# First gate-up of a two-block layer: raw tokens with shift columns for three passes, full modulated tokens after

## What is computed

```python
def modulate(h, shift, scale):
    return h * (1.0 + scale) + shift

def swiglu(h, w_in, w_out):
    gate, up = jnp.split(h @ w_in, 2, axis=-1)
    return (jax.nn.silu(gate) * up) @ w_out

# in the block, with sh_f, sc_f from silu(c) @ w_ada + b_ada:
h = modulate(rms_norm(x, g_pre_ffn), sh_f, sc_f)
x = x + gt_f * rms_norm(swiglu(h, w_ffn_in, w_ffn_out), g_post_ffn)
```

## Time and profile before

| | us |
|---|---|
| median of 3 runs | 965.96 |
| lowest and highest run | 964.58, 970.26 |
| the profiled execution's own time | 967.7 |
| its span in the profile | 965.9 |

### The profile page before, as it was taken

One profiled execution on the slowest core, in us unless ns is written; L12 is line 12 of the kernel. 1 busy time (PEld: TensorE's weight loads), 2 busy tenths in 40 slices (PEclk: granted clock), 3 DMA queues, 4 the chain that ended last, 5 costly groups with the idle time before them and its releaser, 6 DMA issues.

```text
span 965.9 us, 19407 instructions
## 1 busy us (share of the span) xinstructions
PE 951.5 (99%) x7543; PEld 883.8 (92%) x7543; DVE 639.9 (66%) x995; ACT 494.6 (51%) x762; POOL 68.7 (7%) x100
## 2 busy tenths in 40 slices
PE   8999999999999999999999999999999999999997
PEld 3776778899999999899999999999999999999997
DVE  4788886687666765765555546665778766666554
ACT  4765647664454543554444434645665554444531
POOL 0012002200000021000000000200210100000000
PEclk9999999999999999999999999999999999999999
DMA  9972447546666795266666744663445557667741
GB/s 359 400 259 89 131 133 241 185 162 198 183 187 182 207 303 152 67 196 176 179 181 178 224 119 125 214 187 109 129 135 168 160 177 215 188 181 208 220 137 43
DMA packets 189183, 176.06 MB, mean 182 GB/s; under 512 B 7312, under 2 KB 177824, under 8 KB 188752
## 3 DMA queue, kind: packets, MB, share of 16 engines
q1 hardware_dynamic: 183456, 154.29, 52.8%
q0 software_dynamic: 4960, 17.64, 5.2%
q10 hardware_dynamic: 720, 3.49, 0.9%
HBM read 174.32 MB, written 1.05 MB: 182 GB/s over the span
## 4 chain that ended last, share of the span: by engine, by line
PE 85%; DVE 9%; ACT 3%; issue 1%; DMA 1%; SPq 1%; DVEq 0%; ACTq 0%
PE acc L2007 24%; PE acc L2009 23%; PE acc L2008 23%; DVE lo L1143 2%; PE acc L2400 1%; DMA slab_hi<-in_w_ada 1%; PE acc L2205 1%; ACT hi L621 1%; PE acc L2207 1%; PE acc L2206 1%; PE wk L2007 1%; PE acc L2136 1%; PE wk L2009 1%; PE wk L2008 1%; PE wk L2136 1%
## 5 line engine op out<-in xcount | busy, mean ns | idle before, releaser
L1143 DVE TENSOR_TENSOR lo<-raw,hi 128x1024 fp32r<-128x1024 f32 (+1 forms) x259 | 331.0, 1288 | 209.4 <-ACT hi L621 209.1
L621 ACT ACTIVATE hi<-raw 128x1024 fp32r<-128x1024 f32 (+1 forms) x260 | 283.2, 1098 | 130.2 <-PE acc L2009 125.3
L2007 PE MATMUL acc<-n_high,hi 128*128 128x272 f32 (+3 forms) x1016 | 291.2, 287 | 0.5 <-DVE n_low L1958 0.3
L2008 PE MATMUL acc<-n_low,hi 128*128 128x272 f32 (+3 forms) x1016 | 288.1, 284 | 0.0
L2009 PE MATMUL acc<-n_high,lo 128*128 128x272 f32 (+3 forms) x1016 | 288.0, 283 | 0.0
L2007 PEld LDWEIGHTS acc<-n_high,hi 128*128 128x128 f32 (+1 forms) x1016 | 191.7, 189 | 3.0 <-issue 1.4
L2008 PEld LDWEIGHTS acc<-n_low,hi 128*128 128x128 f32 (+1 forms) x1016 | 191.3, 188 | 0.5
L2009 PEld LDWEIGHTS acc<-n_high,lo 128*128 128x128 f32 (+1 forms) x1016 | 191.3, 188 | 0.2
L2007 PE MATMUL acc<-g_high,hi 128*128 128x256 f32 (+1 forms) x528 | 149.2, 283 | 0.0
L2009 PE MATMUL acc<-g_high,lo 128*128 128x256 f32 (+1 forms) x528 | 148.9, 282 | 0.0
L2008 PE MATMUL acc<-g_low,hi 128*128 128x256 f32 (+1 forms) x528 | 148.7, 282 | 0.0
(11 more groups left out here) (428 smaller groups left out, 1246.1 us busy)
## 6 DMA issues: line engine op xcount, KB each, us to landing
raw<-in_w_in SPq DMA_DIRECT2D x52, 512.0 KB, 4.1
raw<-in_w_ffn_in SPq DMA_DIRECT2D x44, 512.0 KB, 3.7
raw<-in_ffn_w_gate SPq DMA_DIRECT2D x44, 512.0 KB, 3.8
raw<-in_ffn_w_up SPq DMA_DIRECT2D x44, 512.0 KB, 3.8
raw<-in_ffn_w_down SPq DMA_DIRECT2D x32, 704.0 KB, 4.5
stage<-in_w_late POOLq DMA_DIRECT2D x24, 512.0 KB, 4.8
raw<-in_w_ffn_out SPq DMA_DIRECT2D x16, 704.0 KB, 5.9
raw<-in_w_out SPq DMA_DIRECT2D x16, 512.0 KB, 4.2
```

Source lines behind the costliest of these rows:

```text
L621: act.activation(hi[:, j, 0:width], raw[:, j, 0:width], ACT.Copy).then_inc(hi_ready, 1)
L1143: dve.tensor_tensor(lo[:, j, 0:width], raw[:, j, 0:width], hi[:, j, 0:width].bitcast(F32), ALU.subtract).then_inc(lo_ready, 1)
L2007: pe.matmul(out_, wH, xH, start=start, stop=False)
L2008: pe.matmul(out_, wH, xL, start=False, stop=False)
```

## The change

In `gu0`, passes 0 to 2 (`RAW_ITS = 3`) stay as they are. From pass 3 on the tokens that are streamed are the full modulated ones, `R * gmod * inv + shift`, 256 columns wide, from `mixH` and `mixL`. They are made in passes 1 and 2: for each of the eight 128-row tiles VectorE makes `R * gmod * inv` in `xg` (`token`), ScalarE adds the shift and rounds (`token_upper`, an Identity with a bias), VectorE makes the lower half (`token_lower`). Passes 3 to 10 then need no column copy, no inverse norm and no bias: ScalarE takes the Silu straight from the accumulator (`gate`), VectorE multiplies (`product`). The engines' orders are written out anew. Since `mixH` and `mixL` are now in use, GpSimd's pieces go to `stage2`, in the memory of the raw tokens, and their first loads wait until pass 2 is done. Counts of `nl_ready`, `sg_ready` and others further on are shifted by constants.

The core of the diff, cut:

```diff
+RAW_ITS = 3
...
-            pool.wait_ge(mm_done, 4 * BASE["gu0"])
+            pool.wait_ge(mm_done, 4 * BASE["gu0"] + 12)
             stage_half(12)
             stage_half(13)
...
+            def token_upper(k):
+                act.wait_ge(xn_ready, KD + k + 1)
+                act.activation(mixH[:, k, :], xg[:, k, 0:T], ACT.Identity, bias=mods[:, 24 + k, 0:1]).then_inc(nh_ready, 1)
...
             def gate_up_shifted(name, ahead):        # ScalarE
...
+                def gate(i):
+                    multiplied(name, i, 1)
+                    act.activation(sg[:, :, 0:T], acc[:, 0:2, 0:T], ACT.Silu).then_inc(acc_free[0], 1)
+
+                def inner_upper(i):
+                    act.wait_ge(acc_free[1], USE[name] + i + 1)
+                    act.activation(inner(g_high, T)[:, ds(2 * i, 2), :], hbuf[:, :, 0:T], ACT.Copy).then_inc(gh_ready, 1)
+
+                for j in (1, 2, 3):
+                    split(first + 1, j, 1024)
+                raw_gate(0)
+                raw_inner(0)
+                for i in (1, 2):
+                    split(first + i + 1, 0, 1024)
+                    token_upper(4 * i - 4)
+                    token_upper(4 * i - 3)
+                    split(first + i + 1, 1, 1024)
+                    raw_gate(i)
+                    split(first + i + 1, 2, 1024)
+                    token_upper(4 * i - 2)
+                    token_upper(4 * i - 1)
+                    split(first + i + 1, 3, 1024)
+                    raw_inner(i)
+                with act.Fori(RAW_ITS + 1, n) as i:
+                    act.activation(warm[:, 7:8], ident[0:1, 0:1], ACT.Silu)
+                    split(first + i, 0, 1024)
+                    split(first + i, 1, 1024)
+                    gate(i - 1)
+                    split(first + i, 2, 1024)
+                    split(first + i, 3, 1024)
+                    inner_upper(i - 1)
...
+            def token(k):
+                dve.scalar_tensor_tensor(out=xg[:, k, 0:T], in0=R[:, k, FRAMES], scalar=gmod[:, k, 2:3], in1=inv[:, 0:T],
+                                         op0=ALU.mult, op1=ALU.mult).then_inc(xn_ready, 1)
+
+            def token_lower(k):
+                dve.wait_ge(nh_ready, 25 + k + 1)
+                dve.scalar_tensor_tensor(out=mixL[:, k, :], in0=xg[:, k, 0:T], scalar=mods[:, 24 + k, 0:1],
+                                         in1=mixH[:, k, :].bitcast(F32), op0=ALU.add, op1=ALU.subtract).then_inc(nl_ready, 1)
+
             def gate_up_shifted(name, ahead):        # VectorE
...
+                def product(i):
+                    multiplied(name, i, 3)
+                    dve.wait_ge(acc_free[0], USE[name] + i + 1)
+                    dve.wait_ge(lo_ready, 4 * (BASE[name] + i) + 5)
+                    dve.tensor_tensor(hbuf[:, :, 0:T], acc[:, 2:4, 0:T], sg[:, :, 0:T], ALU.mult).then_inc(acc_free[1], 1)
+                    inner_lower(i)
+
+                split(first + 1, 1, 1024)
+                raw_gate(0)
+                split(first + 1, 2, 1024)
+                raw_inner(0, lambda: split(first + 1, 3, 1024))
+                for i in (1, 2):
+                    split(first + i + 1, 0, 1024)
+                    token(4 * i - 4)
+                    token(4 * i - 3)
+                    split(first + i + 1, 1, 1024)
+                    token_lower(4 * i - 4)
+                    token_lower(4 * i - 3)
+                    raw_gate(i)
+                    split(first + i + 1, 2, 1024)
+                    token(4 * i - 2)
+                    token(4 * i - 1)
+                    split(first + i + 1, 3, 1024)
+                    token_lower(4 * i - 2)
+                    token_lower(4 * i - 1)
+                    raw_inner(i)
+                with dve.Fori(RAW_ITS + 1, n) as i:
+                    for j in range(4):
+                        split(first + i, j, 1024)
+                    product(i - 1)
...
             def gate_up(name, t0, width, behind, first, steps, operands=(mH, mL), later=None):     # TensorE
...
+                if later:
+                    for s in range(2):
+                        pair(g + 2, USE[name] + 2, s, *xs, width)
+                    xs, width = later, T
+                    pair(g + RAW_ITS, USE[name] + RAW_ITS, 0, *xs, width, (nl_ready, 25, 1))
+                    pair(g + RAW_ITS, USE[name] + RAW_ITS, 1, *xs, width)
+                with pe.Fori(RAW_ITS + 1 if later else 2, COUNT[name]) as i:
```

More of the change, by code:

```diff
@@ L360, in program, with stage_tile @@
         LINEAR_AT = {1: 0, 3: 1}
+        def stage_tile(n, b):
+            side = SLAB_AT[n][0]
+            return stage2[:, 2 * side + b, 0:1024] if n >= 12 else stage[:, 2 * b + 1 - side, :]
         def head_bank(n):
@@ L937, in gate_up_shifted, with raw_gate, raw_inner @@
-                pipeline(name, 1024, evac, ahead, silu=True, behind=((0,), (1,), (), (2, 3)), shifted=True)
+                first, n = BASE[name], COUNT[name]
+                def raw_gate(i):
+                    act.wait_ge(acc_free[0], USE[name] + i + 1)
+                    for m in range(2):
+                        ins = act.activation(sg[:, m, 0:T], sg[:, m, 0:T], ACT.Silu, bias=bcol[:, m, :])
+                    ins.then_inc(sg_ready, 1)
+                def raw_inner(i):
+                    act.wait_ge(hb_ready, i + 1)
+                    act.activation(inner(g_high, T)[:, 2 * i:2 * i + 2, :], hbuf[:, :, 0:T], ACT.Copy).then_inc(gh_ready, 1)
@@ new lines, in gate_up_shifted @@
+                with act.Fori(RAW_ITS + 1, n) as i:
[6 more added lines that the diff above has]
+                    inner_upper(i - 1)
+                split(first + n, 0, ahead[0])
+                gate(n - 1)
+                split(first + n, 1, ahead[1])
@@ L939, in gate_up_scaled @@
+                inner_upper(n - 1)
+                split(first + n, 2, ahead[2])
+                split(first + n, 3, ahead[3])
             def gate_up_scaled(name, f, width, ahead):
@@ L1677, in gate_up_scaled @@
                 pipeline(name, 1024, evac, ahead, peel=True, behind=((0,), (), (), (1, 2, 3)))
-            def gate_up_shifted(name, ahead):
[L1680 to L1703, removed]
@@ L1749, in next_tokens @@
             def next_tokens(k):
-                scaled_lower(25, k, TM, 0, gain(N_F1, k))
+                scaled_lower(33, k, TM, 0, gain(N_F1, k))
             post_norm(3, 4, next_tokens, TM)
@@ L2450, in _, with gate_up @@
             HALVES = [(4 * q + kk, s) for q in range(2) for s in range(2) for kk in range(4)]
-            def gate_up(name, t0, width, behind, first, steps, operands=(mH, mL)):
+            def gate_up(name, t0, width, behind, first, steps, operands=(mH, mL), later=None):
                 xs = (lambda k: operands[0][:, k, t0:t0 + width], lambda k: operands[1][:, k, t0:t0 + width])
@@ L2506, in _ @@
             pe.wait_ge(ada_used, 1)
-            gate_up("gu0", 0, T + 2, lambda: sum_squares(2, T), 17, PACED)
+            gate_up("gu0", 0, T + 2, lambda: sum_squares(2, T), 17, PACED,
+                    later=(lambda k: mixH[:, k, :], lambda k: mixL[:, k, :]))
             down("dn0", 0, T)
```

65 lines of the change are left out of this document (44 added, 21 removed).

## The result

| us | before | after |
|---|---|---|
| median (21 runs each) | 966.17 | 970.04 |
| lowest and highest | 961.71, 970.26 | 966.79, 976.21 |
| the profiled execution's own time | 967.7 | 969.3 |
| its span | 965.9 | 967.4 |

After over before is 1.005 (95% interval 1.0038 to 1.0062), a loss of 3.7 to 6.0 us. The forecast was +7.6: the direction was right, the size too large.

The account below looks back on a forecast made before the run. TensorE, busy 951.5 of 965.9 us, was taken to bound the kernel. Waits 10.1, less 2.3 for width and 0.2 at the down projection, gave +7.6 us: 973.6 on the median, range 966.5 to 979.5.

Parts of the forecast that it names:

- The waits: TensorE idles four times in passes 2 and 3 of the first gate-up, for accumulators and the seventh token: 10.1 us together.
- The chain: VectorE and ScalarE handing to and fro in passes 1 and 2: 16.9 us a pass, against 11.6 for TensorE.
- Work alone fills VectorE: In passes 1 and 2, token instructions add 3.2 to 3.8 us a pass to VectorE's 7.90 busy of 11.60.
- The rival without waits: Engines take ready instructions ahead of blocked ones in the first gate-up, so only the saving is left: 963.5 us; chance 0.07.
- The saving by width: From pass 3 on, 256 columns instead of 258: eight passes of 96 matmuls at 3.0 ns less, 2.3 us.
- The faster-spacing rival: A pause may leave 113.1 ns spacing in passes 4 to 10 and the down projection, gaining 3.2 and 2.5 us: 967.9; chance 0.16.
- The lower clock: Rival: TensorE's clock falls after the two longest waits, 5.8 us for one, 11.6 for both: 979.4 to 985.2; chance 0.12.
- is dense again at once: Argument against the lower-clock rival: the TensorE cover that hides the passes resumes densely right after a wait; no size given.
- The signs named in advance: Right: four idles of 2 to 3 us, 11.3 us passes, splits 3.5 apart. Wrong: no or later idles, 113 spacing, lower clock.
- The Identity with a bias: ScalarE's new token form in passes 1 and 2, 0.51 us each, was charged no table load.
- the moved transfers: GpSimd's four 512 KB weight transfers, moved to the end of pass 2, cost 0; upper bound a load 1 us late.
- the 0.2 at the start of `dn0`: TensorE's 0.2 us wait for the last lower half at the first down projection's start goes, by a shorter last product.

Follow-up runs that it names:

- `gu0` at 256 columns alone: Kernel before with 256 columns in all 11 passes of the first gate-up, shift columns left out, no added work: 962.82 against 967.89 us, ratio 0.9948.
- the last kernel: Changed kernel with all four tokens between gate and third split, plus the loop's product ahead of its last split: 959.68 against 963.27 us, ratio 0.9959.
- the kernel with thin tokens: Changed kernel in its own order, each of the 24 token instructions cut to 2 of 256 columns: 963.34 us in one run.
- the inserted pause: Kernel before, with TensorE starting the first down projection only when its last operand half is written: 968.73 against 963.91 us, ratio 1.0047.
- four tokens in one place: Changed kernel with all four tokens of a pass between gate and third split: 958.6 against 963.91 us (0.9945), then 956.75 against 963.27 (0.996).
- second comparison: Changed kernel run again without an edit, beside the kernel before: 975.36 against 967.89 us, ratio 1.0106.

## Why the prediction was right, and which term was off

**The waits: right in place, releaser and size.** With 1.17 taken from after's times, since its stage began so much later:

| TensorE resumes | predicted | measured | late, predicted | late, measured |
|---|---|---|---|---|
| pass 2 | 223.26 | 223.17 | 1.96 | 1.95 |
| its up half | 231.39 | 231.33 | 2.33 | 2.36 |
| pass 3 | 240.15 | 240.12 | 2.96 | 2.99 |
| its seventh token | 247.21 | 247.22 | 2.81 | 2.73 |

The third is idle time for 1.23; for the other 1.76 the second half of pass 2 took longer, 3.3 us of it at the lower clock. The chain was put at 16.9 us a pass and took 16.94; its first piece was put at 3.53 and took 3.54 (218.07 to 221.61).

**Their cause: half right.** The prediction summed the chain of hand-overs, and that was right. "Work alone fills VectorE" comes near as a share of time, but the work alone makes no wait: in another order it leaves none, with VectorE busy for 9.96 of 10.00 us, and hardly any work in the changed kernel's order leaves 4.7 us idle. The order does it: two tokens stand between two splits, so ScalarE's next split queues behind the tokens' upper halves, which need VectorE's tokens, and VectorE's next split needs ScalarE's. This round trip stands ahead of every multiply that frees an accumulator. The work makes the chain longer, from 4.7 to 7.8 of idle time. The rival without waits needed an engine that overtakes; it falls, as an edit of the order alone takes the waits away. The Trainium skill (TensorE: Matmul & The Clock Gate, Architectural detail: the array is 16× 32×32, not 1× 128×128) says that the queues of ScalarE and VectorE are strictly first in, first out; that agrees.

**The saving by width: the mis-sized term.** It was put at 2.3 for eight passes by taking 117.8 ns as what loops at 256 columns show. After's passes 4 to 10 ran at 113.3 and saved 7 x (11.60 - 10.88) = 5.04, and pass 3 0.3, together 5.35. With 10.0 of waits that is the +4.68 of the stage. In the two other profiles of the changed kernel the spacing was 117.8 and the stage took 7.94 and 7.97 more than before's 129.48, near the forecast's 10.1 - 2.3 = 7.8: with the spacing that it took, the sum for the stage held. The faster-spacing rival named the 113.1, but as something that a pause might leave, and gave it 0.16. The runs show that either value can come, with a pause or without one (113.1 throughout `gu0` at 256 columns alone; 117.9 without a wait in the last kernel). Between the changed kernel's three profiles the passes from 4 on had 113.3, 117.8 and 117.8, and its three medians lie 3.9, 7.5 and 5.5 us above those of before on the same chips, between the rival's +2 and the forecast's +7.6. The forecast priced all runs at the larger value; that this made its median too high fits these profiles, but the spacing of the runs without a profile is not shown.

**The lower clock: it came, and cost nothing.** The rival put 5.8 us on a fall. The clock fell in all three profiles of the changed kernel, once, twice and twice, once in the kernel with thin tokens, and in none of the other kernels' first gate-up. Yet from the stage's start to pass 3's second half they took 52.56, 52.62 and 52.65 us; the waits shrink by what the slower matmuls take (7.8 us idle with one fall, 6.2 with two). What sets pass 3's start is the chain of VectorE and ScalarE, which does not wait for TensorE's clock. So the prediction's reason against a fall, that the cover "is dense again at once", did not hold. The rival's price failed in another step: it added what the lower clock takes to the time, while the next wait was already due and took it up. Where nothing is due, the price is 1.6 us, by the inserted pause. The Trainium skill (same page, The HAM clock gate) says that activity releases the throttle; the falls, each behind one of these waits, agree.

**The signs named in advance came mixed.** The four idle times and the splits 3.5 apart (218.07 to 221.61) came as signs of being right; the pass of 11.3 us came in two of three profiles. Of the signs of being wrong two came as well: 113 from pass 4 in the first profile, and a granted clock of 0.50 near 240 in all three. A time inside the range thus does not decide between the forecast and its rivals: the range took in the faster spacing's 967.9 too, and it held in part because the falls cost nothing.

**Costed at nothing, and right.** The Identity with a bias ran without a table load, two of them in 0.91 us:

```profile
219.72 0.91 ACT L937 ACTIVATE mixH<-xg,mods 128x256 fp32r<-128x256 f32 x2 [1.69 <-DVE xg L1738]
```

No matmul after 248.39 waits in the stage, so the moved transfers and the late splits cost nothing, and the 0.2 at the start of `dn0` went as forecast.

**A better version.** With the tokens between the gate and the third split the idea pays: 0.9945 and 0.996 of the kernel before in two measurements, and on one chip its median was 12 us below that of the changed kernel (956.75 against 968.81).

**Open.** What picks 113.3 or 117.8 ns is not settled. Behind the start of `gu0`'s loops it is constant between two pauses in every profile. A short one can change it: the kernel before begins `dn0` with 33 matmuls 113.8 apart (325.62 to the 329.26 of the earlier trace rows) and goes on at 117.6 behind the 0.28 there, and the first profile with four tokens in one place went from 113.3 to 117.6 at its wait of 0.5.

```profile
325.62 0.28 PE L2007 MATMUL acc<-g_high,hi 128*128 128x256 f32 x1
```

Whether the 0.2 that the change takes out there is what leaves `dn0` at 113.3 in some profiles was not tested. The spacing is worth 3.3 us over passes 3 to 10 and 2.4 over `dn0`, and the sum of 5.7 is near the distance of the two groups of runs of the kernel with four tokens in one place (their means are 956.2 and 962.6); that the groups are this spacing was not seen run by run, since only one run of each kernel has a profile. The three profiles of this order fit: the smaller spacing in the run of 955.72, the larger in those of 964.82 (behind its wait) and 964.78 (the last kernel). Open too is why the changed kernel lost 1.06% in its second comparison and 0.5% in the two others, and why the clock falls once there or twice.

## What to carry to other kernels

When new work is put between the steps of two engines that hand to and fro, count the round trips that come to stand ahead of each instruction that frees a buffer, not the added busy time; the freeing instruction goes first, and the new work goes where the other engine has its data already. A spacing that shows two values in the profile of before belongs on both ends of the range, and a saving is not to be sized by the one that was met more often. A clock that falls inside a chain of waits costs only what the next wait doesn't take up.

## What the runs showed of the hardware

At 256 columns matmuls of this kind ran at 113.3 or 117.8 ns in unchanged code: `gu2` of the kernel before at 117.8 in one profile and at 113.3 in the other. At 258 columns and full granted clock, undisturbed stretches had 120.8 in every profile with that width. The step from 256 to 258 columns was thus worth 3.0 or 7.5 ns, where two of 258 columns' share of 120.8 is 0.9. The Trainium skill (TensorE: Matmul & The Clock Gate, Back-to-back issue gap) gives one sustained value for each of two widths of a stream of weight loads and matmuls; here one width has two.
